# Gated linear attention: rank, key, value and query blocks projected first, gate blocks last and evacuated by ScalarE

## The reference, cut to what matters

```python
proj = h @ w_in
aq, ak, av, bq, bk, bv, br, ba, cq, ck, cv = jnp.split(proj, ...)   # widths 384 x3, 128, 128, 256, 256, 16, 384 x3
# gla(bq, bk, bv, br, ba), 4 heads, key 32, value 64:
log_a = jax.nn.log_sigmoid(ba @ w_a2 + b_a) / 16.0                  # ba: rank 16
# S_t = diag(alpha_t) S_{t-1} + k_t^T v_t,   o_t = q_t S_t,   alpha = exp(log_a)
o = o * rsqrt(mean(o * o) + EPS)
o = o.reshape(...) * norm_w * silu(r)                               # r = br, the gate
```

## Time and profile before

| | us |
|---|---|
| median of 3 runs | 1637.77 (1636.78 to 1639.42) |
| profiled execution, its own time | 1640.32 |
| its span | 1638.5 |
| TensorE busy | 1536.2 (94%) |
| VectorE busy | 928.7 (57%) |
| GpSimd busy | 725.3 (44%) |
| ScalarE busy | 575.7 (35%) |

### The profile page before, as it was taken

The page is one execution under the profiler, slowest core; times in us unless marked ns, Lnnn a source line. Parts: engine busy times, 40 slices in busy tenths (PEclk is TensorE's granted clock), DMA queues, the critical chain, the costliest instruction groups (busy, mean ns, idle before and its releaser), DMA issues.

```text
span 1638.5 us, 21510 instructions
## 1 busy us (share of the span) xinstructions
PE 1536.2 (94%) x6910; PEld 1190.6 (73%) x6910; DVE 928.7 (57%) x1300; ACT 575.7 (35%) x917; POOL 725.3 (44%) x366
## 2 busy tenths in 40 slices
PE   6988967999999999999988999999899999999997
PEld 4765634777888878778766777666687888888885
DVE  5299967368263544786568351666446655564121
ACT  3321255243131323332476332655223323232222
POOL 1589834434444444434323434544243444444442
PEclk7999979999999999999999999999999999999998
DMA  5589820135455555533323324311132333333332
GB/s 190 145 188 198 209 65 27 55 113 167 158 157 166 151 164 153 166 92 86 83 60 93 83 65 104 53 34 39 47 95 64 103 90 102 90 102 89 91 93 86
DMA packets 285060, 176.72 MB, mean 108 GB/s; under 512 B 43794, under 2 KB 269458, under 8 KB 282954
## 3 DMA queue, kind: packets, MB, share of 16 engines
q1 hardware_dynamic: 285002, 175.98, 38.7%
HBM read 173.29 MB, written 5.80 MB: 109 GB/s over the span
## 4 chain that ended last, share of the span: by engine, by line
PE 45%; issue 33%; POOL 11%; DVE 5%; ACT 3%; DMA 2%; SPq 0%; POOLq 0%; DVEq 0%; ACTq 0%
PE ps L1791 13%; PE ps L1793 12%; PE ps L1792 12%; POOL WL L634 9%; DMA vb<-bv_dram 2%; PE ps L2158 2%; PE ps L2001 1%; DVE scanned L1333 1%; PE ps L2169 1%; PE ps L1975 1%; POOL kvp L662 1%; PE ps L2182 1%; DVE qs L1341 1%; ACT LP L883 1%; DVE LP L1395 1%
## 5 line engine op out<-in xcount | busy, mean ns | idle before, releaser
L634 POOL TENSOR_TENSOR WL<-Wraw,WH 128x1024 fp32r<-128x1024 f32 (+2 forms) x239 | 573.1, 2398 | 815.5 <-ACT WH L755 812.0
L1791 PE MATMUL ps<-actH,WH 128*128 128x512 f32 x1256 | 503.9, 401 | 33.3 <-POOL WL L634 14.9
L755 ACT ACTIVATE WH<-Wraw 128x1024 fp32r<-128x1024 f32 (+2 forms) x239 | 246.1, 1031 | 748.8 <-PE ps L1793 658.9
L1792 PE MATMUL ps<-actL,WH 128*128 128x512 f32 x1256 | 493.0, 393 | 0.0
L1793 PE MATMUL ps<-actH,WL 128*128 128x512 f32 x1256 | 492.8, 392 | 0.0
L1791 PEld LDWEIGHTS ps<-actH,WH 128*128 128x128 f32 x1256 | 238.0, 189 | 115.2 <-issue 25.1
L1793 PEld LDWEIGHTS ps<-actH,WL 128*128 128x128 f32 x1256 | 238.0, 189 | 51.2
L1792 PEld LDWEIGHTS ps<-actL,WH 128*128 128x128 f32 x1256 | 238.4, 190 | 48.6 <-issue 1.9
L1791 PE MATMUL ps<-UH,WH 128*128 128x512 f32 x576 | 231.6, 402 | 9.5 <-DVE T L1647 3.9
L1793 PE MATMUL ps<-UH,WL 128*128 128x512 f32 x576 | 228.6, 397 | 0.0
L1792 PE MATMUL ps<-UL,WH 128*128 128x512 f32 x576 | 228.5, 397 | 0.0
(11 more groups left out here) (232 smaller groups left out, 1541.3 us busy)
## 6 DMA issues: line engine op xcount, KB each, us to landing
Wraw<-in_w_ff SPq DMA_DIRECT2D x64, 512.0 KB, 4.1
Wraw<-in_w_in SPq DMA_DIRECT2D x56, 512.0 KB, 4.0
wada<-in_w_ada SPq DMA_DIRECT2D x64, 384.0 KB, 4.2
Wraw<-in_w_up SPq DMA_DIRECT2D x44, 512.0 KB, 3.8
vb<-bv_dram SPq DMA_DIRECT2D x64, 256.0 KB, 4.6
Wraw<-in_w_down SPq DMA_DIRECT2D x16, 448.0 KB, 3.8
Wraw<-in_w_proj_rnn SPq DMA_DIRECT2D x16, 320.0 KB, 3.1
Wraw<-in_w_proj_mla SPq DMA_DIRECT2D x8, 512.0 KB, 4.1
```

Source lines behind the costliest of these rows:

```text
L634: nc.gpsimd.tensor_tensor(WL[slot][:, 0:kts, :], Wraw[slot][:, 0:kts, :], WH[slot][:, 0:kts, :].bitcast(F32), ALU.subtract).then_inc(s_lo, 1)
L755: A(WH[slot][:, 0:kts, :], Wraw[slot][:, 0:kts, :], ACT.Copy).then_inc(s_hi, 1)
L1791: MM(o, wh, ah, start=first, stop=False)
L1792: MM(o, wh, al, start=False, stop=False)
```

## The change

The order of the seven `gB` blocks becomes rank, key, value, value, query, gate, gate (`B_ORDER`). The gate factor is computed as soon as the rank block is out, between the copies of the following blocks, and its instructions on ScalarE stand between the high halves of blocks 3 and 4. VectorE copies only the first five blocks out; the last two are evacuated by ScalarE with Silu, straight from PSUM, and these two instructions stand behind the high half of the first `gQK` block. On SyncE the store of the values stands before the loads of the first two `gQK` blocks instead of behind them. On GpSimd the low halves of the first two `gQK` blocks are no longer made ahead: the order is products of group g, then low half of block g, and the low halves of blocks 16 and 17 come after all groups. On TensorE the sums of group g are in block g+1 instead of g+2, and the last block has none.

```diff
+B_ORDER = (6, 1, 2, 3, 0, 4, 5)
 # SyncE
+            def b_load(n):
+                slot = gB.slot(n)
+                load(gB.n0 + n, slot, [(Wraw[slot][:], w_in[:, :, COL_B + P * B_ORDER[n]:COL_B + P * (B_ORDER[n] + 1)])])
-            qk_load(0, 0, 0)
-            qk_load(1, 0, 1)
             sp.wait_ge(s_ev, gB.b0 + 4)
             sp.dma_start(bv_dram.rearrange("(k p) t -> p k t", p=P), bT[:, 2:4, :]).then_inc(S("bv_stored"), 16)
...
             gla_values(0, 0)
             gla_values(1, 1)
-            qk_load(2, 0, 2)
-            qk_load(3, 0, 3)
-            gla_values(2, 0)
...
+            for n in range(qk_blocks + PAIRS):
+                qkv_load(n)
+                if 1 <= n < GLA_GROUPS - 1:
+                    gla_values(n + 1, (n + 1) % 2)
 # GpSimd
-            lows(gQK, 2, 1)
             def gla_round(i):
                 for j in range(2):
                     gla_products(2 * i + j, j)
-                    low(2 * i + (gQK.n0 + 2 + j), gQK.slot(j))
+                    low(2 * i + (gQK.n0 + j), gQK.slot(j))
             peeled(pool, GLA_GROUPS // 2, gla_round)
+            for n in range(GLA_GROUPS, 3 * PAIRS):
+                low(gQK.n0 + n, gQK.slot(n))
 # ScalarE
-            highs(gB, 2, NB_B // 2 - 1, first=2)
-            highs(gB, 1, 1, first=NB_B - 1)
-            highs(gQK, 2, 1)
-            act.wait_ge(s_ev, gB.b0 + NB_B)
+            highs(gB, 2, 1, first=2)
             act.wait_ge(S("gla_zmin"), 1)
             own.done(A(T[1][:], ps[:, 2, :], ACT.Abs, bias=...))
             own.done(A(T[1][:], T[1][:], ACT.Exp, scale=-1.0))
             A(T[1][:], T[1][:], ACT.Ln, bias=ones[:, 0:1]).then_inc(S("gla_log"), 1)
             act.wait_ge(S("gla_logsig"), 1)
             A(gla_decay, T[0][:], ACT.Exp, scale=1.0 / B_TAU).then_inc(S("gla_alpha"), 1)
-            A(bT[:, 4:6, :], bT[:, 4:6, :], ACT.Silu).then_inc(S("gla_silu"), 1)
+            highs(gB, 2, 1, first=4)
+            highs(gB, 1, 1, first=NB_B - 1)
+            highs(gQK, 1, 1)
+            for e in range(2):
+                n = NB_B - 2 + e
+                act.wait_ge(s_mm, gB.n0 + n + 1)
+                act.wait_ge(s_ev, gB.b0 + n)
+                A(bT[:, 4 + e, :], ps[:, gB.bank(n), :], ACT.Silu).then_inc(s_ev, 1)
+            highs(gQK, 1, 1, first=1)
 # VectorE
+            b_evac(0)
+            b_evac(1)
             dve.wait_ge(S("gla_z"), 1)
             V.tensor_scalar(T[0][:], ps[:, 2, :], vcol("gla_b_a"), 0.0, ALU.add, ALU.min)...
+            b_evac(2)
             dve.wait_ge(S("gla_log"), 1)
             V.tensor_tensor(T[0][:], T[0][:], T[1][:], ALU.subtract)...
+            b_evac(3)
+            b_evac(4)
+            dve.wait_ge(s_ev, gB.b0 + 5)
+            own.done(V.tensor_scalar(gla_query, bT[:, 0, :], float(B_KEY ** -0.5), None, ALU.mult))
 # TensorE
             pair_product(gB, gB.n0, x_in, n1, lambda j: [], lag=LAG)
+            pe.wait_ge(s_ev, gB.b0 + 1)
+            MM(ps[:, 2, :], wa2[:], bT[0:B_RANK, NB_B - 1, :], start=True, stop=True).then_inc(S("gla_z"), 1)
             products(gB, 2, NB_B // 2 - 1, x_in, first=2)
             products(gB, 1, 1, x_in, first=NB_B - 1)
-            pe.wait_ge(s_ev, gB.b0 + NB_B)
-            MM(ps[:, 2, :], wa2[:], bT[0:B_RANK, NB_B - 1, :], start=True, stop=True).then_inc(S("gla_z"), 1)
...
+            for n in range(2 * PAIRS):
+                block_product(gQK, gQK.n0 + n, n, 0, x_in, 0, None, free(gQK.b0 + n), gla_sums(n - 1, (n - 1) % 2) if n else None)
             for v in range(PAIRS):
-                block_product(gV, ..., gla_sums(2 * PAIRS - 2 + v, v % 2))
+                block_product(gV, ..., gla_sums(2 * PAIRS - 1 + v, (v + 1) % 2) if v < PAIRS - 1 else None)
```

More of the change, by code:

```diff
@@ L415, in _ @@
             w_in = wcols("w_in", 0, KT)
-            b_cols = cols(w_in, KT, lambda i, j: 2 * P * i + (COL_B + P * j))
-            stream(gB, 2, 1, b_cols)
+            def b_load(n):
+                slot = gB.slot(n)
+                load(gB.n0 + n, slot, [(Wraw[slot][:], w_in[:, :, COL_B + P * B_ORDER[n]:COL_B + P * (B_ORDER[n] + 1)])])
+            b_load(0)
+            b_load(1)
             for g, names in enumerate(VEC_GROUPS):
@@ L433, in _ @@
             sp.dma_start(tab_dram, tabs[:]).then_inc(S("tab_stored"), 16)
-            stream(gB, 2, 1, cols(w_in, KT, lambda i, j: COL_B + 2 * P + P * j), first=2)
+            b_load(2)
+            b_load(3)
             sp.wait_ge(S("tab_stored"), 16)
@@ L438, in _, with qkv_load @@
                          ).then_inc(S("strips_stored"), 16)
-            stream(gB, 2, NB_B // 2 - 2, cols(w_in, KT, lambda i, j: 2 * P * i + (COL_B + 4 * P + P * j)), first=4)
-            stream(gB, 1, 1, cols(w_in, KT, lambda i, j: COL_B + P * (NB_B - 1)), first=NB_B - 1)
+            for n in range(4, NB_B):
+                b_load(n)
             bases = (COL_AQ, COL_AK, COL_CQ, COL_CK)
[L444 to L450, removed]
-            qk_load(0, 0, 0)
-            qk_load(1, 0, 1)
+            qk_blocks = 4 * PAIRS // 2
+            def qkv_load(n):
+                if n < qk_blocks:
+                    at = bases[n % 4] + P * (n // 4)
+                else:
+                    at = (COL_AV, COL_CV)[n % 2] + P * ((n - qk_blocks) // 2)
+                slot = gQK.slot(n)
+                load(gQK.n0 + n, slot, [(Wraw[slot][:], w_in[:, :, at:at + P])])
             sp.wait_ge(s_ev, gB.b0 + 4)
@@ L1305, in _, with b_evac @@
                        lambda k: actH[:, k, :])
[L1307 to L1310, removed]
+            def b_evac(n):
+                dve.wait_ge(s_mm, gB.n0 + n + 1)
+                V.tensor_copy(bT[:, B_ORDER[n], :], ps[:, gB.bank(n), :]).then_inc(s_ev, 1)
+            b_evac(0)
+            b_evac(1)
             dve.wait_ge(S("gla_z"), 1)
             V.tensor_scalar(T[0][:], ps[:, 2, :], vcol("gla_b_a"), 0.0, ALU.add, ALU.min).then_inc(S("gla_zmin"), 1)
+            b_evac(2)
             dve.wait_ge(S("gla_log"), 1)
             V.tensor_tensor(T[0][:], T[0][:], T[1][:], ALU.subtract).then_inc(S("gla_logsig"), 1)
+            b_evac(3)
+            b_evac(4)
+            dve.wait_ge(s_ev, gB.b0 + 5)
+            own.done(V.tensor_scalar(gla_query, bT[:, 0, :], float(B_KEY ** -0.5), None, ALU.mult))
             dve.wait_ge(S("gla_alpha"), 1)
@@ L1373, in _ @@
                 dve.wait_ge(S("gla_turned"), e + 1)
-                dve.wait_ge(S("gla_silu"), 1)
+                dve.wait_ge(s_ev, gB.b0 + NB_B)
                 dve.wait_ge(S("v_turned"), PAIRS)
@@ L1954, in _ @@
             for v in range(PAIRS):
-                block_product(gV, gV.n0 + v, v, 0, x_in, 0, None, free(gV.b0 + v), gla_sums(2 * PAIRS - 2 + v, v % 2))
+                block_product(gV, gV.n0 + v, v, 0, x_in, 0, None, free(gV.b0 + v),
+                              gla_sums(2 * PAIRS - 1 + v, (v + 1) % 2) if v < PAIRS - 1 else None)
                 if v:
                     turn_values(v - 1)
-                if v == 1:
+                if v == 0:
                     turn_sums(0)
```

## The result

The changed kernel takes 1645.37 us in the median of its five runs (1644.89 in that of the four that count), the kernel before 1639.16: ratio 1.0039, with a 95% interval of 1.0025 to 1.0053, 6.4 us slower (2.5 to 5.3 thousandths of 1638 us are 4.1 to 8.7 us). Three runs are left out of all ratios as slow ones: one of 5335.76 us here, one of 5335.82 us of `one_key` and one of 1928.33 us of `one_key_again`. The forecast was 1644.9, with 1641.0 to 1648.5 around it.

A forecast was written before the change was run, and what follows sets the result against it. VectorE was taken as the bound from 90 to 207 us, TensorE's queue at the stage's end. Tail 13.1 - head 7.9 + wait 1.5 + loop 0.4 = +7.1 us on the median 1637.77: 1644.9, range 1641.0 to 1648.5.

The forecast's parts named there:

- The tail: TensorE's end: blocks 15, 16, 17 and transpositions take 19.9 us instead of 6.79, adding 13.1 us.
- The head: Start of VectorE's chain: store issued 7.9 us earlier, second group's scans at 82.0 us; gain 7.9, bounds 6.5 to 9.
- I keep the distances of the earlier trace: SyncE's queue after the store: same broadcasts and weight load in the same order, so products start at 68.9 us.
- The signs that hung on the head: VectorE's last reading near 201 us, blocks without idle time up to 217.5 to 219, attention some 7 us later.
- The clock and the wait for sums: TensorE idles 7.7 us, restarts at 1.2 GHz; VectorE waits 1.5 us in group 2, bounds 0 to 4.
- The loop: Each later group's reading needs sums from block g-1, 4.78 us against 4.79 to 4.83: 0.4 us in total, 0 to 3.
- Ports: VectorE's own products against GpSimd on SBUF: a changed phase could be worth -4 to +5 us; not in the sum.
- Ports fall well: Rival, VectorE's own products: changed phase against GpSimd saves 4.1 us, so +3, 1641 us; chance 10%.
- Faster: the stage ends with VectorE's chain: Rival, 199 to 212 us: last two blocks go under VectorE's chain, whole 7.9 us kept, 1629.9 us; chance 5%.
- The loop binds: Rival, VectorE's readings: waits of 0.2 to 0.4 us in most groups, +10 to +12, about 1649 us; chance 10%.
- the head doesn't move: Rival, start of the chain: the store is still late, +13, 1651 us; chance 3%.
- No wait for sums: Rival, TensorE's restart: clock returns sooner or the loop has slack, +5.2, 1643.0 us; chance 17%.

The follow-up runs named there:

- one_key: `one_ahead` with VectorE's own product in groups 1 to 11 reading the key from a copy in PSUM bank 6: ratio 0.9975 to the kernel before.
- one_key_again: `one_key` unaltered, measured again beside `two_key` and `key_only`: ratio 0.9976 to the kernel before.
- reweave_only: Kernel before with only the new weave on GpSimd and TensorE, gate factor and store still late: ratio 1.0068, 1651.19 us against 1636.97.
- key_only: Kernel before with one edit, VectorE's product in groups 1 to 11 reading the key from a PSUM copy: ratio 0.9983.
- early_only: Changed kernel with the weave two blocks ahead as before and the store behind the first two query and key loads: ratio 1.0004 to the kernel before.
- one_ahead: Changed kernel with the first query block's low half made before group 0, its load issued during the store's landing: ratio 0.9989 to the kernel before.
- two_ahead: `early_only` with the store issued before the first two query and key loads: ratio 0.9983 to the kernel before.
- two_key: `two_ahead` with the key in PSUM for groups 1 to 11: ratio 0.9952 to the kernel before, medians 1631.76 and 1638.58 us.
- cq_first: Changed kernel with the order of query and key blocks turned from A, A, C, C to C, C, A, A: single run 1644.35 us.
- clock: Changed kernel plus 24 matmuls with unused result on TensorE before the first query block: single run 1639.33 us.
- again: The changed kernel unaltered, measured once more: ratio 1.0027 to the kernel before.
- before_look: The kernel before unaltered, run for a second trace: 1641.35 us.

## Why the prediction was right, and where it was not

**The tail: right, to a tenth.** 19.9 us were forecast from block 15 to the transposition, and 19.92, 19.87 (`reweave_only`) and 12.77 for the version with one block less were measured. TensorE never idled in it. Two blocks that used to be done before the chain stand behind it. `reweave_only` shows this part without the early head, 11 us slower.

**The head: right in its mechanism, under-sized.** "I keep the distances of the earlier trace rows" is the step that was off. The second group's scans came 10.7 us earlier, not 7.9, and outside the stated bounds of 6.5 to 9. Of the 2.8 us, 0.7 is that the whole stage began earlier in this execution; 0.6 is the landing of the store (4.6 instead of 5.2 us); 1.4 is the weight load behind the broadcasts: ScalarE started on it 9.8 us after its issue, where the earlier trace rows have 11.2. The signs that hung on the head were missed with it: the last reading came at 197.45 (201 forecast), the last transposition at 214.36 (217.5 to 219), the attention 3.1 us later than before (7).

What makes that load faster stays open. From its issue to ScalarE's start it is 9.8, 10.0, 9.65 and 10.05 us in the four profiles with the changed kernel's order of loads, where the next load is issued 0.5 us behind it. It is 11.2 in both profiles of the kernel before, in `key_only` and in `early_only`, where the next load comes 1.6 to 2.1 us later. But it is 10.4 in `one_ahead`, and 9.7 and 10.7 in the two profiles of one and the same kernel, `one_key` and `one_key_again`, with the next load 5.4 us later, and 11.2 and 10.75 in `two_ahead` and `two_key` with 5.9 us. So neither the next load's place nor the columns (`cq_first`) sort these times, and one kernel can differ from itself by 1 us.

**The clock and the wait for sums: right in the mechanism, somewhat over-sized.** Forecast 1.5 us, measured 1.21, 0.78 and (`cq_first`) 0.35. `clock` shows that it was the low clock: with the engine kept busy it is nothing. The rows of TensorE for 80 to 84 us in these three profiles (the granted clock is the third number from the right) go with it, the later the clock is back, the longer the wait:

```profile
80.00:84.00 4.00, 4.00 (x14) 0.67 0.80 166
80.00:84.00 4.00, 4.00 (x16) 0.80 0.72 154
80.00:84.00 4.00, 4.00 (x16) 0.87 0.78 166
```

TensorE idled 5.6 us and not 7.7, since the head came sooner.

**The loop: over-sized.** 0.4 us was put in for later groups. The readings there take 0.65 to 0.69 us instead of 0.66 and none waits. The 4.78 against 4.83 us was enough.

**Ports: the unknown term that I left at zero.** The eight products took 10.8 us in the first profile of the changed kernel against 9.9 before, but 9.0 against 9.1 in the second profiles of the two. In the other kernels that read the key from SBUF they took 9.2 to 11.5. So this term moves by 1.7 us between two executions of one kernel, and no part of it can be put down to the change. *Ports fall well* asked for 4 us less and did not come.
The Trainium skill (SBUF — State Buffer, the part on two separate sides) gives the rule behind it: two SBUF inputs on VectorE against a GpSimd instruction that reads SBUF. `one_key` agrees: 683 ns with one of them in PSUM, 1788 without.

**The sum.** For the first pair of profiles 13.13 - 10.66 + 1.21 + 0.84 = +4.5 us for the stage end, against the measured 3.1. Of the 1.4 between them 1.0 is VectorE's product in the last group (1.70 us, before 0.72), for which the low half of block 15 does not wait; 0.4 I have not traced. For the second pair (`again`, `before_look`) 13.09 - 10.16 + 0.78 - 0.04 = +3.7 us, measured 3.5. These sums still hold the earlier start of the stage, which isn't the change's. By length the stage is 3.2 to 4.5 us longer, whichever two profiles are paired, and what follows it is not (1412.6 and 1414.9 us before, 1411.2 and 1411.6 after). That fits the 4.4 and 6.4 us of the two measurements, with intervals of 2 us to either side.

So +7.1 was too much, by 2 us of head, 0.3 to 1.1 us of wait and 0.4 us of loop, all in one direction. It lies inside the interval of the first measurement only. That the time came out within 0.5 us of the forecast is in part luck: the median that the forecast started from, 1637.77 us of three runs, was 1639.16 with two more.

**The rivals.** "Faster: the stage ends with VectorE's chain" fell: VectorE ended 8.9 us earlier and waited 18.5 us for TensorE. "The loop binds" and "the head doesn't move" fell as well. "No wait for sums" is `clock`: the wait is worth 0.35 to 1.2 us, and without it the stage of the changed kernel is still longer than before (188.64 us against 185.55 and 184.91).

## What to carry to other kernels

When two streams of work are woven on several engines, an earlier start of the one is only a gain if the other does not lose its lead: count the blocks that stand behind the last group, since each was paid in full here (7.2 us with sums and transposition, 5.6 without sums), and fill the wait at the head with them. `one_ahead` and `two_ahead` do that, and neither is slower than the kernel before. Where VectorE and GpSimd both work from SBUF, giving VectorE's instruction one operand from PSUM kept it at 0.68 us, where it took up to 1.9 us when it met GpSimd, and GpSimd's own next instruction was 0.4 us shorter too. A distance between two events that hangs on transfers in flight should not be carried over to a new order of transfers without a bound of its own.

## What was not expected of the hardware

Executions of one and the same kernel go with TensorE's mean granted clock: of 73 runs of the kernel before beside these experiments, on two chips, the 7 at 0.978 have a median of 1635.7 us, the 9 at 0.974 one of 1638.7, the 7 at 0.970 one of 1643.5. That is 8 us between runs without any change of the program, more than the change itself, and it is why the intervals here are 2 us wide with up to 12 runs. Whether the clock makes the time or only goes with it, no run here tests.

And the mutual exclusion of VectorE and GpSimd is exact enough to be read off a timeline: 0.55 us from the end of the one to the end of the other, 67 times out of 67.
